# Emptying the key and query tiles of two expansions by VectorE and ScalarE together

## What is computed

```
q_c = (rmsnorm(cq, cq_g) @ w_uq).reshape(B, S, C_HEADS, C_NOPE + C_ROPE)       # 256 -> 8 x (64 + 32)
q_nope = q_c[..., :C_NOPE]
q_rope = apply_rope(q_c[..., C_NOPE:], cos_c, sin_c)
kv = (rmsnorm(ckv, ckv_g) @ w_ukv).reshape(B, S, C_HEADS, C_NOPE + C_V)        # 128 -> 8 x (64 + 64)
k_nope, v_c = kv[..., :C_NOPE], kv[..., C_NOPE:]
k_rope = apply_rope(kr[:, :, None, :], cos_c, sin_c)[:, :, 0]                  # shared by the heads
yc = mla_attention(q_nope, q_rope, k_nope, k_rope, v_c) * jax.nn.silu(gc)
zc = yc @ w_oc
```

## Time and profile before

| | us |
|---|---|
| three timed runs | 1025.59, 1026.84, 1027.16 |
| their median | 1026.84 |
| the profiled execution, its own time | 1027.14 |
| its span, first to last instruction | 1025.2 |
| TensorE busy (97% of the span) | 998.0 |
| VectorE busy (61%) | 629.9 |
| ScalarE busy (40%) | 408.8 |

### The profile page before, as it was taken

The page is one execution under the profiler, slowest core; times in us unless marked ns, Lnnn a source line. Parts: engine busy times, 40 slices in busy tenths (PEclk is TensorE's granted clock), DMA queues, the critical chain, the costliest instruction groups (busy, mean ns, idle before and its releaser), DMA issues.

```text
span 1025.2 us, 13123 instructions
## 1 busy us (share of the span) xinstructions
PE 998.0 (97%) x5116; PEld 790.0 (77%) x5116; DVE 629.9 (61%) x1098; ACT 408.8 (40%) x769; POOL 0.2 (0%) x4
## 2 busy tenths in 40 slices
PE   7999999999999999999999999999999999999994
PEld 5887877888777877688888787778877787767883
DVE  6556457646658586666556555584564766765844
ACT  5343233424533255533334323342364324554323
POOL 0000000000000000000000000000000000000000
PEclk9999999999999999999999999999999999999998
DMA  6333321222225311123223332122212432111212
GB/s 238 105 101 113 124 84 62 99 86 83 78 87 144 103 62 42 42 83 103 82 82 120 97 102 104 65 101 92 94 64 81 143 104 82 42 54 54 100 42 82
DMA packets 28207, 92.99 MB, mean 91 GB/s; under 512 B 3745, under 2 KB 3873, under 8 KB 28018
## 3 DMA queue, kind: packets, MB, share of 16 engines
q1 hardware_dynamic: 25008, 87.04, 25.2%
q10 hardware_dynamic: 3138, 5.11, 1.9%
HBM read 86.31 MB, written 3.28 MB: 87 GB/s over the span
## 4 chain that ended last, share of the span: by engine, by line
PE 91%; DVE 5%; ACT 2%; issue 1%; DMA 1%; SPq 0%; DVEq 0%; ACTq 0%
PE ring L525 73%; PE nat L525 5%; PE nat L652 3%; PE nat L662 3%; PE nat L689 2%; PE nat L675 1%; DMA raw<-pieces 1%; ACT w_hi L711 1%; DVE w_lo L987 1%; PE nat L616 1%; PE nat L638 1%; PE aux L622 1%; PE nat L604 0%; DVE gates L1330 0%; DVE merged L965 0%
## 5 line engine op out<-in xcount | busy, mean ns | idle before, releaser
L525 PE MATMUL ring<-act_hi,w_hi 128*128 128x512 f32 x864 | 359.2, 416 | 5.7 <-DVE w_lo L987 2.9
L525 PE MATMUL ring<-act_hi,w_lo 128*128 128x512 f32 x864 | 338.0, 391 | 0.0
L525 PE MATMUL ring<-act_lo,w_hi 128*128 128x512 f32 x864 | 337.9, 391 | 0.0
L711 ACT ACTIVATE w_hi<-raw 128x1024 fp32r<-128x1024 f32 x154 | 162.6, 1057 | 373.9 <-PE ring L525 342.6
L987 DVE TENSOR_TENSOR w_lo<-raw,w_hi 128x1024 fp32r<-128x1024 f32 x154 | 187.5, 1219 | 57.4 <-ACT w_hi L711 57.3
L525 PEld LDWEIGHTS ring<-act_hi,w_hi 128*128 128x128 f32 x864 | 162.6, 188 | 53.1 <-issue 14.2
L525 PEld LDWEIGHTS ring<-act_lo,w_hi 128*128 128x128 f32 x864 | 162.8, 188 | 35.3 <-issue 4.3
L525 PEld LDWEIGHTS ring<-act_hi,w_lo 128*128 128x128 f32 x864 | 162.6, 188 | 35.3
L1220 DVE SCALAR_TENSOR_TENSOR gates<-ring,rstd 128x512 f32<-128x512 f32 x72 | 49.7, 690 | 134.5 <-PE ring L525 134.2
L525 PE MATMUL ring<-y_hi,w_hi 128*128 128x512 f32 x192 | 74.9, 390 | 1.1 <-issue 1.1
L525 PE MATMUL ring<-y_hi,w_lo 128*128 128x512 f32 x192 | 74.7, 389 | 0.0
(11 more groups left out here) (171 smaller groups left out, 979.4 us busy)
## 6 DMA issues: line engine op xcount, KB each, us to landing
raw<-pieces SPq DMA_DIRECT2D x154, 512.0 KB, 3.4
xt<-x_t SPq DMA_DIRECT2D x4, 512.0 KB, 7.4
bank_a<-work SPq DMA_DIRECT2D x32, 64.0 KB, 2.0
rope<-tables SPq DMA_DIRECT2D x1, 1024.0 KB
bank_g<-k_rope_dram ACTq DMA_DIRECT2D x2, 512.0 KB, 4.3
q_rope_dram<-work ACTq DMA_DIRECT2D x4, 256.0 KB, 2.3
bank_a<-q_rope_dram ACTq DMA_DIRECT2D x4, 256.0 KB, 5.4
out_t<-gates SPq DMA_DIRECT2D x4, 256.0 KB, 2.3
```

Source lines behind the costliest of these rows:

```text
L525: mm = pe.matmul(dst, stationary, moving, start=start and i == 0, stop=stop and i == 2)
L711: nc.scalar.activation(w_hi[:, n % HL, :], raw[:, n % RAW, :], ACT.Copy).then_inc(hi_split.sem, 1)
```

## The change

Each bank of keys or plain queries is read by both engines at once: VectorE copies partitions 0 to 63 (the even head) and ScalarE partitions 64 to 127 (the odd head). That holds for the odd outputs of PUKV, for output 2 of PUQ and for all three outputs of PUQ+1. Values and the rotary part are read as before. A new `shared(p, o)` names the outputs with two readers; each reader signals on its own counter, and TensorE waits for both before it writes such a bank again (`emptied_by`). Nothing changes in `SCHEDULE`, in the matmuls, in the DMAs or in the number of bytes copied.

```
+def shared(p, o):
+
+    return (p == PUKV and o % 2 == 1) or (p, o) == (PUQ, 2) or p == PUQ + 1
+
+
 def act_reads(p, o):
 
-    return (p == PUKV and o % 2 == 0) or (p, o) in ((PUQ, 2), (PUQ + 1, 1))
+    return p == PUKV or shared(p, o)
 
 
 def by_dve(r):
 
-    return r - by_act(r)
+    return r - sum(first_output(PUKV) + o < r for o in range(0, 8, 2))
+
+
+def emptied_by(r):
+
+    for p in (PUKV, PUQ, PUQ + 1):
+        o = r - first_output(p)
+        if 0 <= o < outputs_of(p):
+            return not act_reads(p, o) or shared(p, o), act_reads(p, o)
+    return True, False
...
                         if start:
-                            if by_act(r - 2) > by_act(r - 3):
+                            by_vector, by_scalar = emptied_by(r - 3)
+                            if by_scalar:
                                 pe.wait_ge(ring_act.sem, ring_act.at(layer, by_act(r - 2)))
-                            else:
+                            if by_vector:
                                 pe.wait_ge(proj_free.sem, proj_free.at(layer, by_dve(r - 2)))
...
                                 nc.scalar.activation(v_c[:, o // 2, :], ring[(first_output(p) + o) % 3][:, :],
                                                      ACT.Copy).then_inc(ring_act.sem, 1)
+                                if o == 0:
+                                    act.wait_ge(read_done.sem, read_done.at(layer, 4))
+                                act.wait_ge(proj_done.sem, proj_done.at(layer, signals_before(p) + o + 2))
+                                nc.scalar.activation(k_c[0:64, o + 1, :], ring[(first_output(p) + o + 1) % 3][64:128, :],
+                                                     ACT.Copy).then_inc(ring_act.sem, 1)
                         if p in (PUQ, PUQ + 1):
-                            o, h = (2, 0) if p == PUQ else (1, 4)
-                            act.wait_ge(proj_done.sem, proj_done.at(layer, signals_before(p) + o + 1))
-                            r = ring[(first_output(p) + o) % 3]
-                            nc.scalar.activation(q_c[0:64, h, :], r[0:64, :], ACT.Copy)
-                            nc.scalar.activation(q_c[0:64, h + 1, :], r[64:128, :], ACT.Copy).then_inc(ring_act.sem, 1)
+                            for o in ((2,) if p == PUQ else range(3)):
+                                h = 0 if p == PUQ else 2 * (o + 1)
+                                act.wait_ge(proj_done.sem, proj_done.at(layer, signals_before(p) + o + 1))
+                                nc.scalar.activation(q_c[0:64, h + 1, :], ring[(first_output(p) + o) % 3][64:128, :],
+                                                     ACT.Copy).then_inc(ring_act.sem, 1)
...
                             for o in range(1, 8, 2):
                                 evacuated(layer, p, o + 1)
-                                r = ring[(first_output(p) + o) % 3]
-                                h = o - 1
-                                nc.vector.tensor_copy(k_c[0:64, h, :], r[0:64, :])
-                                nc.vector.tensor_copy(k_c[0:64, h + 1, :], r[64:128, :]).then_inc(proj_free.sem, 1)
+                                nc.vector.tensor_copy(k_c[0:64, o - 1, :], ring[(first_output(p) + o) % 3][0:64, :]
+                                                      ).then_inc(proj_free.sem, 1)
...
-                            for o in (() if p == PUQ else (0, 2)):
+                            for o in ((2,) if p == PUQ else range(3)):
                                 evacuated(layer, p, o + 1)
-                                r = ring[(first_output(p) + o) % 3]
                                 h = 0 if p == PUQ else 2 * (o + 1)
-                                nc.vector.tensor_copy(q_c[0:64, h, :], r[0:64, :])
-                                nc.vector.tensor_copy(q_c[0:64, h + 1, :], r[64:128, :]).then_inc(proj_free.sem, 1)
+                                nc.vector.tensor_copy(q_c[0:64, h, :], ring[(first_output(p) + o) % 3][0:64, :]
+                                                      ).then_inc(proj_free.sem, 1)
```

## The result

| | before | after |
|---|---|---|
| median, us | 1026.96 (6 runs, 1025.49 to 1027.28) | 1029.90 (6 runs, 1028.27 to 1032.80) |
| profiled execution, us | 1027.14 | 1028.27 |
| its span, us | 1025.2 | 1026.3 |
| ratio after to before | | 1.0038, 95% interval 1.0026 to 1.0050 |

The changed kernel is slower by 2.9 us in the medians. The ratio and its interval go by all runs and not by the medians, whose ratio is 1.0029; by the means the loss is 3.8 us. The forecast was 1030.4, from 1.96 us of later starts and one fall of TensorE's clock.

What follows compares the result with a forecast made beforehand. TensorE, busy 97% of the span, was taken to bound the kernel. To 1026.84 us before, 1.96 for later PO[1] starts and 1.6 for one drop of TensorE's clock gave 1030.4 us, range 1028.0 to 1032.2.

Steps and rivals of the forecast that it cites:

- The keys: In PUKV, key tiles copied by both engines free their banks earlier, so PUQ starts 1.1 us sooner per layer.
- The rotary chain: After PUQ starts, the first rotary product L1298 and all rotary work behind it move 1.1 us forward too.
- The saves in the way: ScalarE's PUQ+1 copy queues behind its wait for query rotary rows sent to DRAM: PO[1] 1.06 and 0.90 us later.
- Its signs: At PO[1], TensorE waits over 2 us, ended by ScalarE's query copy, itself behind the sends to DRAM.
- The wait behind VectorE for tile 2 of PUQ: At PUQ+1's third tile, TensorE waits some 0.3 us for VectorE's copy behind L1305, which does not matter.
- Two waits at one start: TensorE waiting on both engines' counters before a shared bank was priced at nothing, at most 0.8 us.
- rival (A): Both engines reading one shared bank go one after the other: 1030.8 us, more if the clock drops; chance 0.05.
- Part 2(c): PO[1]'s second output needs ScalarE's copy of PUQ+1's tile 1, ending 2.7 us before it is asked for; no cost.
- The clock: After idle times of 2.4 and 2.2 us ahead of PO[1], TensorE's clock drops once of two chances: 1.6 us.
- The guess from the spread of the three times of before: Their 1.57 us spread would fit if the one known clock drop near the start does not happen each run.
- B: TensorE's clock holds after both idle times ahead of PO[1]: 1028.8 us, chance 0.30.
- C: TensorE's clock drops after both idle times ahead of PO[1]: 1032.0 us, chance 0.18.

Runs made afterwards that it cites:

- keys alone: Against the changed kernel, query tiles copied as before the change and only key tiles shared by both engines: 1024.76 us, ratio 0.9980 to before.
- before with the start filled: The kernel before plus 4 unused matmuls of 256 columns in TensorE's 2.9 us idle time near the start of layer 0: 1025.59 us.
- queries-only kernel: Against the changed kernel, key tiles copied as before the change and only query tiles shared by both engines: 1031.19 us, ratio 1.0038 to before.

## Why the prediction was right, step by step

**The keys.** Predicted 1.1 us a layer, measured 1.05 at PUQ (3.80 against 4.85) and 1.13 with keys alone. Tile 4 was expected 0.91 behind tile 3 and came at 0.99.

**The rotary chain.** Predicted to move with PUQ: L1316 was expected 6.74 us behind tile 3 (310.95 - 304.21) and came at 6.72 (309.42 - 302.70).

**The saves in the way.** The main step, that ScalarE's copy of tile 0 of PUQ+1 stands behind the wait, is shown by three kernels: it is in the profile, it goes when the wait moves, and the start of PO[1] follows the saves' length. Its signs came, though TensorE's stands, expected at 2.4 and 2.2 us, were 1.98 and 1.96. Its size was a little high, 1.06 and 0.90 us predicted, 0.66 and 0.63 measured. The term that was mis-sized is the saves, taken at 2.94 us as in the earlier trace rows and measured at 2.75 and 2.74, and in layer 0 the fetches' issue, 0.99 taken and 0.82 measured. The prediction had named the reason why the saves might gain (a raw transfer that starts later in relation to them) and set it at nothing. The profiles bear it out. Where VectorE's order around the saves is that of before, SyncE issues the next raw transfer 1.13 us behind the first save (317.05 and 315.92 before the change), and all six pairs of saves, in before, keys only and before with the start filled, took 2.93 to 2.98 us. Where VectorE copies tile 2 of PUQ ahead of the split, the transfer comes 1.72 us behind (314.99 and 313.27 after), and nine of ten pairs of saves, in five kernels that wait for them, took 2.74 or 2.75. The tenth is the 3.29 of the queries-only kernel, which has the same 1.72 and is not explained. No run tested the transfer by itself.

**The small terms.** The wait behind VectorE for tile 2 of PUQ is there (0.3 us, inside the later stand) and did not matter. Two waits at one start cost nothing that shows: PUQ begins 12 matmuls behind tile 4 in 2.81 us, 0.234 each. Two engines in one bank cost nothing: 0.68 and 0.60 us, together, at 306.70. This rival (A) is out. The Trainium skill, "PSUM — Partial Sum Buffer", section "PSUM bank collisions raise a hardware error", says that two engines may access different quadrants of one bank at the same time; the trace agrees, with the 0.68 and 0.60 us above. Part 2(c) had tile 1's copy of PUQ+1 end 2.7 us before it is asked for; by its own times it is some 2.2, and the copy was in time.

**The clock.** One fall of two was taken, 1.6 us. The medians give: 2.94 us of loss, 1.3 of it the later starts and some 1.6 the clock, and filling the two stands takes 1.57 away. So the size was right in the medians. That the count came out at one is in part luck: by the means (3.8 us) the six runs had some 1.5 falls more than before, and the queries-only kernel, with stands as long or longer, never had more than one in all in five runs. The ground for it was thinner than the prediction says. It took the chance of a fall for a matter of length between 1.8 and 2.89 us; the profiles show stands of 1.98 with a fall and 1.96 without in one execution, and stands of 2.52, 2.85 and 2.90 without. So length within 1.9 to 2.9 us does not tell which stand brings one. The guess from the spread of the three times of before has become a finding: it is the fall at the start.

The total came out 0.5 us under the forecast: 0.7 too much for the later starts, less the 0.1 by which the median of before rose (1026.84 to 1026.96) and less than 0.1 in the clock. Rivals B (no fall behind the new stands) and C (two) gave times that single runs had, but not always for their reason. All ten profiles fit a count of falls wherever they lie, 1.4 to 1.6 us each over the level of their kernel without any, and that level of the changed kernel is about 1026.8. The run at 1028.27 is the profiled one: it had a fall behind PO[1], against B, and none at the start. By this count the three runs near 1029.9 had two falls and the one at 1031.49 three; 1032.80 is more than three falls give and was not looked into. The range's upper end, 1032.2, is called the upper side of C, but 1032.0 with the 0.7 us would be 1032.7.

## What to carry to other kernels

When a bank's emptying is split over two engines, the slower of the two queues decides, not the slower copy: look at what stands ahead of the new copy on its engine, above all a wait for a transfer. Put a round trip's second half, the wait and the fetch, behind the work that others are waiting for. Here a TensorE wait of two or three microseconds cost its length and, in part of the runs, a fall of the clock on top; a few unused matmuls ahead of the wait took that away.

## What the runs showed of the hardware

- A fall of TensorE's clock to the 1.2 GHz level costs 1.6 us when the matmuls behind it are dense, the distance going from 0.23 to 0.43 us. It followed stands of 1.98 us (once) and of 2.86 to 2.90 (four times) in five of the ten profiles and did not follow stands of 1.95 to 2.90 in others. In the four kernels without the start's and PO[1]'s long stands, stands of 1.0 to 1.2 us remained, with one ahead of 10 us that was as long as 1.88 and 2.14 in two of the profiles, and none of their 38 runs lies 1.6 us above the lowest of its kernel. This is what the two levels of this kernel's times are.
- ScalarE and VectorE read disjoint partitions of one PSUM bank at the same time at full pace (0.60 and 0.68 us for 64x512 fp32).
- ScalarE's copy out of PSUM takes as long for 64 partitions as for 128 (both 0.60 us), VectorE's 64x512 copy 0.68. So half of a tile costs ScalarE a whole tile's time. Splitting can pay here because the two heads go to the same partitions of SBUF and need two copies in any case.
- Two saves of 256 KB from SBUF to DRAM took 2.74 to 3.29 us from the first issue to the first fetch behind the wait.
